# Hybrid SSD + pooling block with a top-4-of-32 mixture of experts, one core: the tail behind the experts as straight code on TensorE, the last scatter ahead of the weight copy, the residual reloaded ahead of the gain

## The reference, cut to what matters

```python
x = x + (g_ssd * y_ssd + g_pool * y_pool) @ w_mix_out[i]
h = rms_norm(x, ffn_norm_g[i])
x = x + moe_ffn(h, ...)                 # top 4 of 32 experts per token, 512 tokens
ple_gate = jax.nn.sigmoid(rms_norm(x, ple_norm_g[i]) @ w_ple_gate[i])
x = x + ple_gate * (p[i] @ w_ple_proj[i])
return rms_norm(x, final_norm_g)
```

## Time and profile before

| | us |
|---|---|
| median of 3 runs | 1851.38 |
| lowest and highest run | 1849.42, 1852.15 |
| the profiled execution's own time | 1840.45 |
| its span, first to last instruction | 1838.7 |
| PE busy | 1800.7 (98%) |
| DVE busy | 1409.7 (77%) |
| ACT busy | 1177.0 (64%) |
| POOL busy | 414.1 (23%) |

### The profile page before, as it was taken

How to read it: one execution, slowest core, us unless ns; L and a number is a source line. 1 busy time by engine, 2 the same in 40 slices (tenths; PEclk the granted TensorE clock), 3 DMA queues, 4 the chain that set the end, 5 groups by cost and what they waited for, 6 DMA issues and landing times.

```text
span 1838.7 us, 25521 instructions
## 1 busy us (share of the span) xinstructions
PE 1800.7 (98%) x8997; PEld 1495.9 (81%) x8997; DVE 1409.7 (77%) x1027; ACT 1177.0 (64%) x936; POOL 414.1 (23%) x324
## 2 busy tenths in 40 slices
PE   7999999999999999999999999999999999999998
PEld 6888888677889978888888888888888888888876
DVE  4576776563334689889899899989988988989974
ACT  4655455342223577777777777777777777777765
POOL 5223334530000412212212211221221221221100
PEclk9999999999999999999999999999999999999999
DMA  6433443333337299999999999999999999999951
GB/s 186 122 107 104 115 126 98 115 124 88 97 112 294 72 381 369 380 368 373 375 370 376 374 369 388 374 368 388 369 374 379 378 377 367 375 375 368 375 179 46
DMA packets 153768, 504.50 MB, mean 274 GB/s; under 512 B 15690, under 2 KB 76146, under 8 KB 120084
## 3 DMA queue, kind: packets, MB, share of 16 engines
q1 hardware_dynamic: 141684, 478.50, 69.7%
q0 software_dynamic: 11984, 25.22, 5.8%
q10 hardware_dynamic: 48, 0.07, 0.0%
HBM read 493.67 MB, written 26.30 MB: 283 GB/s over the span
## 4 chain that ended last, share of the span: by engine, by line
PE 87%; DVE 4%; POOL 3%; ACT 3%; issue 2%; DMA 0%; SPq 0%; DVEq 0%; POOLq 0%; ACTq 0%
PE gu_ps L2112 25%; PE gu_ps L2116 12%; PE dn_ps L2127 12%; PE gu_ps L1880 7%; PE gu_ps L1882 7%; PE gu_ps L1881 7%; PE dn_ps L2133 6%; PE et_ps L2098 3%; PE gu_ps L2283 1%; PE dn_ps L2283 1%; ACT w_hi L911 1%; PE gu_ps L1902 1%; PE gu_ps L2187 1%; POOL win L814 1%; POOL dx L800 1%
## 5 line engine op out<-in xcount | busy, mean ns | idle before, releaser
L1696 DVE TENSOR_TENSOR split_l<-ring,split_h 128x2048 fp32r<-128x2048 f32 x384 | 868.2, 2288 | 91.3 <-ACT split_h L1177 89.4
L1177 ACT ACTIVATE split_h<-ring 128x2048 fp32r<-128x2048 f32 x384 | 727.0, 1917 | 145.5 <-PE gu_ps L2116 112.7
L2112 PE MATMUL gu_ps<-split_h,xgT_h 128*128 128x512 f32 x992 | 272.6, 397 | 1.2 <-DVE xgT_l L1702 1.2
L2116 PE MATMUL gu_ps<-split_l,xgT_h 128*128 128x512 f32 x992 | 265.8, 390 | 0.0
L2112 PE MATMUL gu_ps<-split_h,xgT_l 128*128 128x512 f32 x992 | 265.7, 390 | 0.0
L2112 PEld LDWEIGHTS gu_ps<-split_h,xgT_l 128*128 128x128 f32 x992 | 186.2, 188 | 39.5
L2116 PEld LDWEIGHTS gu_ps<-split_l,xgT_h 128*128 128x128 f32 x992 | 186.3, 188 | 39.2
L2112 PEld LDWEIGHTS gu_ps<-split_h,xgT_h 128*128 128x128 f32 x992 | 181.6, 188 | 43.2 <-issue 8.3
L1356 DVE TENSOR_TENSOR w_lo<-w_raw,w_hi 128x2048 fp32r<-128x2048 f32 (+1 forms) x45 | 103.2, 2293 | 143.7 <-ACT w_hi L911 130.4
L827 POOL COPY icur<-slots 128x1 int32 (+1 forms) x31 | 52.5, 1692 | 622.6 <-PE et_ps L2098 622.6
L2127 PE MATMUL dn_ps<-split_h,actT_h 128*128 128x512 f32 x496 | 155.6, 395 | 0.0
(11 more groups left out here) (358 smaller groups left out, 2625.5 us busy)
## 6 DMA issues: line engine op xcount, KB each, us to landing
ring<-in_w_gate_up SPq DMA_DIRECT2D x256, 1024.0 KB, 7.2
ring<-in_w_down SPq DMA_DIRECT2D x128, 1024.0 KB, 7.7
w_raw<-in_w_in SPq DMA_DIRECT2D x28, 1024.0 KB, 5.9
arow<-acum_rows POOLq DMA_DIRECT2D x16, 512.0 KB, 6.4
w_raw<-in_w_ssd_out SPq DMA_DIRECT2D x8, 1024.0 KB, 5.9
w_raw<-in_w_in SPq DMA_DIRECT2D x9, 512.0 KB, 6.3
w_raw<-in_w_mix_out SPq DMA_DIRECT2D x4, 1024.0 KB, 8.8
wpg<-in_w_ple_gate SPq DMA_DIRECT2D x2, 2048.0 KB, 20.4
```

Of the source, the lines that this page charges most:

```text
L1177: a.activation(split_h[s % SPLIT][:, :], ring[s % RING][:, :], ACT.Copy).then_inc(hi_done, 1)
L1696: v.tensor_tensor(split_l[s % SPLIT][:, :], ring[s % RING][:, :], split_h[s % SPLIT][:, :].bitcast(F32), ALU.subtract).then_inc(lo_done, 1)
L2112: t.matmul(gu_ps[:, b * 512:b * 512 + 512], x[:, k, :], split_h[s][:, b * 512:b * 512 + 512], start=False, stop=False)
L2116: o = t.matmul(gu_ps[:, b * 512:b * 512 + 512], xgT_h[:, k, :], split_l[s][:, b * 512:b * 512 + 512], start=False, stop=k == KD - 1)
```

## The change

On PE the test is turned round: `If(rows <= P)` with the tail as its body, and an `Else` with passes 1 to 3 and a second copy of the tail. On POOL `scatter` issues the indirect DMA first and copies the next weights behind it; the 31st scatter no longer waits for its landing; POOL loads the register and makes its test first, waits for the landing behind it, and then signals `moe_end` (inside the `If` it waits and frees `y_sb` ahead of the passes). On SP the four reloads of the residual stand ahead of the load of `ogain`. ACT and DVE are unchanged.

```diff
@@ -718,10 +718,10 @@
             sp.wait_ge(moe_end, 1)
-            sp.dma_start(ogain[:, :], final_norm_g.partition_broadcast(P)).then_inc(ogain_loaded, 16)
             sp.wait_ge(last_mm, 1)
             for c in range(CH):
                 sp.dma_start(x2[c][:, :], x1_rows[c * P:c * P + P, :]).then_inc(x_loaded[c], 16)
+            sp.dma_start(ogain[:, :], final_norm_g.partition_broadcast(P)).then_inc(ogain_loaded, 16)
@@ -844,12 +844,10 @@
-            def scatter(n, col, steps, following=None):
+            def scatter(n, col, steps, following=None, landed=True):
 
                 pool.wait_ge(y_evac, n + 2)
                 alone(pool)
-                if following is not None:
-                    weigh(following)
                 g.tensor_copy(dcur[:, :], col).then_inc(idx_done, 1)
                 pool.wait_ge(idx_done, steps)
                 alone(pool)
@@ -857,8 +855,11 @@
                                      oob_is_err=False, compute_op=ALU.add
                                      ).then_inc(y_stored, 16)
-                pool.wait_ge(y_stored, 16 * n + 16)
-                pool.sem_inc(y_free, 1)
+                if following is not None:
+                    weigh(following)
+                if landed:
+                    pool.wait_ge(y_stored, 16 * n + 16)
+                    pool.sem_inc(y_free, 1)
@@ -881,7 +882,8 @@
                 for e in range(NE - 3, NE - 1):
-                    scatter(j * NE + e, slots[:, e:e + 1, 0], k0 + NE + e + 1, slots[:, e + 1:e + 2, 1].bitcast(F32))
+                    scatter(j * NE + e, slots[:, e:e + 1, 0], k0 + NE + e + 1, slots[:, e + 1:e + 2, 1].bitcast(F32),
+                            not isinstance(j, int) or e < NE - 2)
@@ -890,10 +892,16 @@
             pool.wait_ge(route_done, 1)
-            for j in passes(pool):
-                pool.wait_ge(et_done, j * PASS_T)
-                scatter(j * NE - 1, slots[:, NE - 1:NE, 0], j * 2 * NE)
-                one_pass(j)
+            rows = pool.value_load(maxcount[0:1, 0:1], min_val=0, max_val=SEQ)
+            with pool.If(rows > P):
+                pool.wait_ge(y_stored, 16 * (NE - 1))
+                pool.sem_inc(y_free, 1)
+                with pool.Fori(1, PASSES) as j:
+                    pool.wait_ge(et_done, j * PASS_T)
+                    scatter(j * NE - 1, slots[:, NE - 1:NE, 0], j * 2 * NE)
+                    one_pass(j)
+            pool.nop()
+            pool.wait_ge(y_stored, 16 * (NE - 1))
             pool.sem_inc(moe_end, 1)
@@ -2236,11 +2244,6 @@
             one_pass(0)
-            pe.wait_ge(route_done, 1)
-            for j in passes(pe):
-                one_pass(j)
-
-            t.transpose(et_ps[:, 0:P], ident[:, :], ident[:, :]).then_inc(last_mm, 1)
@@ -2296,47 +2299,59 @@
-            pe.wait_ge(p_low, 2)
-            embed(0)
...
+            def ending():
+
+                t.transpose(et_ps[:, 0:P], ident[:, :], ident[:, :]).then_inc(last_mm, 1)
+                pe.wait_ge(p_low, 2)
+                embed(0)
...
+            pe.wait_ge(route_done, 1)
+            rows = pe.value_load(maxcount[0:1, 0:1], min_val=0, max_val=SEQ)
+            with pe.If(rows <= P):
+                ending()
+            with pe.Else():
+                with pe.Fori(1, PASSES) as j:
+                    one_pass(j)
+                ending()
```

More of the change, by code:

```diff
@@ L2297, in embed @@
                 o.then_inc(pp_mm, 1)
-            pe.wait_ge(p_low, 2)
-            embed(0)
[L2301 to L2329, removed]
-                        for h in range(2):
[L2331 to L2339, removed]
+            def ending():
+                t.transpose(et_ps[:, 0:P], ident[:, :], ident[:, :]).then_inc(last_mm, 1)
+                pe.wait_ge(p_low, 2)
+                embed(0)
+                embed(1)
+                embed(2)
+                pe.wait_ge(share_done, 1)
+                for c in range(CH):
+                    o = t.transpose(bank[1][0:3 * NE, c * P:c * P + P],
+                                    share3[:, c, :, :].rearrange("p m e -> p (m e)"), ident[:, :])
+                o.then_inc(share_turned, 1)
+                embed(3)
+                pe.wait_ge(share_low, 2)
+                pe.wait_ge(placed, 1)
+                put_back(0)
+                pe.wait_ge(pp_read, 2)
+                put_back(1)
+                pe.wait_ge(pp_read, 4)
+                turned_x2(0)
+                put_back(2)
+                for i in range(4, 2 * CH):
+                    embed(i)
+                pe.wait_ge(pp_read, 6)
+                put_back(3)
+                pe.wait_ge(pp_read, 8)
+                for c in range(CH):
+                    if c < 2:
+                        pe.wait_ge(x2_done, DONE[2 * c + 2])
+                    pe.wait_ge(x2T_low, DONE[c] + 1)
+                    if c >= 2:
+                        pe.wait_ge(pg_read, c - 1)
+                    if c < CH - 1:
+                        for k in range(KD):
+                            for h in range(2):
+                                o = gate(c, k, h)
+                            if k == 3:
+                                turned_x2(c + 1)
+                        o.then_inc(pg_done, 1)
+                    else:
+                        for h in range(2):
+                            for k in range(KD):
+                                o = gate(c, k, h)
+                            o.then_inc(pg_done, 1)
```

## The result

| | before | changed |
|---|---|---|
| median of 20 runs each, us | 1852.13 | 1854.12 |
| lowest and highest | 1849.42, 1854.87 | 1852.25, 1857.26 |
| ratio, 95% interval | | 1.0012 [1.0007, 1.0018] |
| the profiled execution: its time, its span | 1840.45, 1838.7 | 1853.37, 1851.6 |
| tail: from the end of the last y_sb to the end of the span | 85.98 | 87.13 |

The kernel became 2.0 us slower (1.3 to 3.3 by the interval).

The account below looks back on a forecast made before the run. PE was taken to bound the kernel, including the tail of about 78 us. Gap -3.20 plus wait for pT_l +4.14 gives +0.94 us: 1841.4 profiled, plus 10.9 to the median, 1852.3 us; range 1848.0 to 1855.5.

Parts of the forecast that it names:

- PE's branch: PE ahead of the tail: straight code removes the 5.83 us taken branch, 3.20 us of it on the path.
- ACT's wait for the last weight copy: ACT ahead of pj_h: w_ready comes 4.27 us late, at 1758.36, so embed(0) starts 0.94 us later.
- POOL's prices: 31st scatter on POOL: dcur 0.17 us, DMA 3.25, weight copy 1.20; their bounds move embed(0) by -0.1 to +4.1 us.
- The first 30 scatters cost nothing: Loop scatters: copying the weight behind the DMA costs nothing, as ACT needs it some 35 us later and POOL idles 20.85.
- The reload: First residual reload on SP: issued 2.9 us sooner, 5.5 us to landing, there at 1770.9; DVE comes at 1775.15, gaining nothing.
- rival A: w_ready is not late, the copy running beside the DMA's descriptor work; the reload binds, gain 3.3 us, 1848.1; chance 0.13.
- The clock: PE behind the gap: same stretch at 1.2 GHz as before; bounds zero more and 1.4 us more or less.
- The range: Whole kernel: 1848.0 to 1855.5 us, from POOL's bounds and the clock's 1.4 us, lowered to rival A's 1848.1.
- The detour in the chain of before: Short detour over DVE in the tail's chain of waits: the residual's reload must be there before the addition at 1774.21.
- Rival C: POOL's last weight copy behind the DMA waits for program code: +6.8 us, 1858.2; chance 0.08 together with POOL's upper ends.

Follow-up runs that it names:

- first pair of profiles: One profiled execution each of the unedited kernels: before 1840.45 us, tail 85.98; changed 1853.37 us, tail 87.13.
- second pair: Both kernels profiled once more, unedited, on another chip: tail 85.62 before, 88.55 changed; the changed kernel's ratio 1.0013.
- copy first in the 31st: Changed kernel with the weight copy ahead of the DMA again in the 31st scatter alone; 1848.15 us, ratio to the kernel before 0.9977.
- the first four experiments: Weight copy first in the 31st scatter (ratio 0.9977); only the scatter's order changed (1.0013); only PE's straight tail (1.0007); ACT's wait at its use (0.9981).

## Why the prediction was right, point by point

- **PE's branch.** Forecast: the stall of 5.83 us goes, the test stays. Shown: 74 ns. The new jump at the end was priced at up to 5.83 us, hidden; it took 3.66 us, hidden. The Trainium skill (Runtime: NRT & Kernel Launch, Instruction fetch mechanics) says that a taken branch beyond the loaded blocks waits for a fetch. The 3.66 us agree with it; no run here shows the fetch itself.
- **ACT's wait for the last weight copy.** This was the step that made the forecast, and it holds: w_ready 5.77 us behind the last y_sb against the forecast 5.64, pT_l at 12.23 against 12.09, embed(0) at 12.29 against 12.12. Two experiments that remove it in different ways gain 4.5 to 4.8 us in the tail, one that lengthens it by 7.46 us costs 8.0.
- **POOL's prices** were each wrong, and their sum right by luck. "I take 0.17" for dcur: it took 1.21 us in the 31st scatter and 1.16 in the loop. So the scatter went out 0.12 us sooner, not 1.14. Of the two copies the one that stands first behind ACT's y_sb bears the 1.2 us, whatever its type: wcur before, dcur in the changed kernel. And "what stands behind one starts at its end": the copy started 2.79 us behind the DMA's start, ahead of the end of its 3.36 us, and took 0.77, not 1.20. The errors are +1.04 for dcur, -0.46 for the start behind the DMA (2.79 instead of 3.25) and -0.43 for the copy: +0.15 together, against w_ready 0.13 us later than forecast.
- **The first 30 scatters cost nothing.** Right: 1051.0 against 1051.1 us.
- **The reload.** Forecast: issued 2.9 us sooner and of no use in the changed kernel. It was issued 2.2 us sooner (13.34 against 15.57), landed in 3.5 us instead of 5.5, and was of no use there: DVE added at once when its own work was done. The forecast kept the 5.5 us of a load that stood behind the gain vector, though the change put it in front. Where embed(0) starts near 7.8 and the reload lands late, DVE waits for it, as rival A said.
- **The clock.** "so I assume the same stretch at 1.2 GHz behind it" is the term that was mis-sized. The stretch isn't the same from one execution to the next: the eighteen matmuls took 5.73 and 4.19 us in the two profiles of before and 5.82 and 6.73 in the two of after. Nor does it cost the two kernels the same: before, the reload lay close behind it, so that going without the slow clock brought only 0.34 us; in the changed kernel filling the gap gave back 1.5 and 2.5 us. In the first pair of profiles the forecast holds nearly to the number (embed(0) +1.11, tail +1.15 us). In the second pair embed(0) is 1.72 us later, 0.47 of it ACT's slower register load, and the tail is 2.9 us longer; the remaining 1.2 us are the clock's 2.5 in the matmuls, less most of the 1.37 us that the kernel before waited for its reload anyway. Between them lie the +2.0 of the medians, so that the right mechanism and the sign were shown, and +0.9 was half of the size.
- **The range.** Its lower end takes 1.4 us off for the clock, its upper end of 1855.5 holds POOL's prices alone; with the clock's 1.4 it is 1856.9. And 0.75 us of the distance from the predicted 1852.3 to the measured 1854.12 is the kernel before, whose median is 1852.13 over 20 runs against the 1851.38 that the sum started from.
- **The detour in the chain of before** was read as the reload's, ahead of the addition at 1774.21. The reload had landed by 1773.8; what DVE finished last there was its own work, the low parts of shareT and of the gate weights. The chain of "copy first in the 31st" passes the same way.
- **Rival A** (w_ready not late) was given 3.3 us and its experiment has 4.8 in the tail, 3.9 in the median: the size was off since the reload lands in 3.4 us there, with no other load issued ahead of it, not in 5.5. Then DVE's own work binds, at 16.68. That experiment has the weight copied first; the rival's own form, a copy beside the DMA, is nearer to what happened (the copy began ahead of the end of the DMA's row), but it wasn't early enough.
- **Rival C** (POOL fetches code): no copy took more than 2.3 us. The page's 6 us for a freshly loaded program (the Trainium skill, GPSIMD Engine Reference, 2.1 Instruction dispatch) don't show up on a copy in either order; no trace here shows the loading of such a program.

## What to carry to other kernels

Before a stall is removed, list what stands ready at its end: here a chain over three engines was ready just when PE ran dry, and a wait written for the loop's sake (a semaphore awaited at the end of a pass, five operations of the same engine ahead of its use) turned a 4.4 us later copy into a later matmul. A wait belongs directly ahead of the use. On a queue with a dependent load behind it, what isn't needed yet goes last: one 512 KB load ahead of the critical one cost 3.6 us in one execution, of which 1.5 was the slow clock behind the gap that it opened, and perhaps half of that by the medians.

## What the runs showed of the hardware that was not expected

- **A gap on PE costs more than its length, and not always.** Gaps of 2.4, 3.2, 4.3, 4.4, 4.8 and 11.8 us were followed by matmuls at a granted clock of 0.50, worth 1.5 to 2.5 us; one of 3.08 us was not. The longest of them cost 2.2 us.
- **POOL's indirect DMA looks shorter when a copy stands behind it.** In the loop DMA_INDIRECT took 3.71 us before and 1.61 us in the changed kernel, where the weight copy starts 1.05 us behind its start; landing took 9.5 us in the median instead of 11.7. In the 31st scatter it isn't so: the row is 3.36 us with a copy behind it that starts 2.79 us behind its start, and 3.24 to 3.36 us in the kernels where only a wait follows. What the engine does in that time, and why the 31st differs, stays open. It moved nothing here, as the landing is covered in the loop.
- **DVE stood still for 9.1 us around 625 us** in the profile of the changed kernel and of the first four experiments, and in none of the other profiles: not in the kernel before (twice), not in the changed kernel the second time. The trace names no releaser ("remote"). PE and ACT then wait for DVE; POOL goes on with its indirect DMAs at the same pace as in the profile without the standstill. The first four experiments ran on one chip, on which the kernel before has its median at 1852; on the chip of the others it has 1840. Since the changed kernel lacks it in its second profile, it is not the change's. With the slow clock behind it (PE at 0.50 until about 643 us) it makes up the 11.8 us by which the first profile of the changed kernel lags behind the second from there on. That it explains the 12 us between the medians is likely, but no profile of the kernel before shows it: the first, at 1840.45 us, lies below all twenty runs of its set (1849.42 and up), and the second is from the other chip. Its cause stays open.
